# The opening of a two-block transformer kernel: pairs of feature blocks against one block at a time

## The reference, cut to what matters

```
mod = silu(c) @ w_mod + b_mod          # 6 x 1024: shift, scale, ... for x
mc  = silu(c_ctx) @ w_mod + b_mod      # the same for ctx
h   = rmsnorm(x, g_mix)   * (1 + mod[1]) + mod[0]
hc  = rmsnorm(ctx, g_mix) * (1 + mc[1])  + mc[0]
f   = h  @ w_in[:, 0:1024]             # forget gates of x, forward and backward
fc  = hc @ w_in[:, 0:1024]             # forget gates of ctx
```

## Time and profile before

| | |
|---|---|
| Time, median of 3 runs (lowest to highest) | 1463.91 us (1463.87 to 1466.01) |
| The profiled execution's own time | 1463.74 us |
| Its span (first to last instruction) | 1462.5 us |
| TensorE busy | 1433.3 us, 98% of the span |
| VectorE, ScalarE busy | 856.6 us (59%), 755.1 us (52%) |
| DMA | 267.34 MB, mean 183 GB/s |
| Mean granted clock of TensorE | 0.997 of full |

### The profile page before, as it was taken

The page is one execution under the profiler, slowest core; times in us unless marked ns, Lnnn a source line. Parts: engine busy times, 40 slices in busy tenths (PEclk is TensorE's granted clock), DMA queues, the critical chain, the costliest instruction groups (busy, mean ns, idle before and its releaser), DMA issues.

```text
span 1462.5 us, 19657 instructions
## 1 busy us (share of the span) xinstructions
PE 1433.3 (98%) x8098; PEld 1205.4 (82%) x8098; DVE 856.6 (59%) x1191; ACT 755.1 (52%) x1086; POOL 22.9 (2%) x72
## 2 busy tenths in 40 slices
PE   7999999999999999999999999999999999999998
PEld 5999889978888788888897888887888879888886
DVE  4628766875554755556355655557555475755553
ACT  4435355555453655445565655446455476755442
POOL 0000000000000000000121000000000000000000
PEclk9999999999999999999999999999999999999999
DMA  9437666555555555555433555565555552355552
GB/s 382 153 102 300 240 232 215 175 171 185 186 187 189 196 185 185 185 191 192 165 116 123 177 183 183 187 194 188 185 184 187 185 182 73 116 184 186 190 186 89
DMA packets 69930, 267.34 MB, mean 183 GB/s; under 512 B 7760, under 2 KB 8016, under 8 KB 66384
## 3 DMA queue, kind: packets, MB, share of 16 engines
q1 hardware_dynamic: 67680, 259.13, 52.7%
q10 hardware_dynamic: 2160, 6.95, 1.4%
HBM read 265.00 MB, written 1.05 MB: 182 GB/s over the span
## 4 chain that ended last, share of the span: by engine, by line
PE 91%; DVE 5%; ACT 2%; DMA 1%; issue 1%; SPq 0%; POOL 0%; DVEq 0%; ACTq 0%
PE PS L728 24%; PE PS L744 14%; PE PS L746 14%; PE PS L745 14%; PE PS L371 5%; PE PS L373 4%; PE PS L372 4%; PE PS L712 2%; PE PS L403 1%; PE PS L404 1%; PE PS L405 1%; DMA MC<-in_mod 1%; PE PS L472 1%; DVE WL L1652 1%; DVE TN L2099 1%
## 5 line engine op out<-in xcount | busy, mean ns | idle before, releaser
L1652 DVE TENSOR_TENSOR WL<-RAW,WH 128x1024 fp32r<-128x1024 f32 (+1 forms) x440 | 532.0, 1221 | 330.0 <-ACT WH L1093 329.5
L1093 ACT ACTIVATE WH<-RAW 128x1024 fp32r<-128x1024 f32 (+1 forms) x440 | 454.2, 1054 | 299.7 <-DMA RAW<-in_up 178.6
L744 PE MATMUL PS<-WH,XH 128*128 128x512 f32 (+1 forms) x928 | 380.9, 410 | 9.2 <-DVE XL L2107 9.0
L746 PE MATMUL PS<-WH,XL 128*128 128x512 f32 (+1 forms) x928 | 362.1, 390 | 0.0
L745 PE MATMUL PS<-WL,XH 128*128 128x512 f32 (+1 forms) x928 | 361.7, 390 | 0.0
L744 PEld LDWEIGHTS PS<-WH,XH 128*128 128x128 f32 x928 | 174.3, 188 | 59.5 <-DVE XL L2107 13.9
L746 PEld LDWEIGHTS PS<-WH,XL 128*128 128x128 f32 x928 | 174.2, 188 | 37.2
L745 PEld LDWEIGHTS PS<-WL,XH 128*128 128x128 f32 x928 | 175.0, 189 | 27.7
L728 PE MATMUL PS<-WH,GH 128*128 128x512 f32 x440 | 137.3, 393 | 0.0
L728 PE MATMUL PS<-WL,GH 128*128 128x512 f32 x440 | 135.8, 390 | 0.0
L728 PE MATMUL PS<-WH,GL 128*128 128x512 f32 x440 | 135.6, 389 | 0.0
(11 more groups left out here) (344 smaller groups left out, 1821.6 us busy)
## 6 DMA issues: line engine op xcount, KB each, us to landing
RAW<-in_up SPq DMA_DIRECT2D x220, 512.0 KB, 4.7
RAW<-in_down SPq DMA_DIRECT2D x110, 512.0 KB, 3.2
RAW<-in_win SPq DMA_DIRECT2D x44, 512.0 KB, 6.2
RAW<-in_mod SPq DMA_DIRECT2D x16, 1024.0 KB, 6.8
MC<-in_mod SPq DMA_DIRECT2D x8, 1024.0 KB, 13.6
RAW<-in_sbqk SPq DMA_DIRECT2D x16, 512.0 KB, 4.7
GROW<-in_grow ACTq DMA_DIRECT2D x9, 512.0 KB, 4.6
RAW<-in_wo SPq DMA_DIRECT2D x8, 512.0 KB, 4.1
```

Source lines behind the costliest of these rows:

```text
L744: e.matmul(o_[:, 0:n], l, w[:, s], start=(k == 0), stop=False, skip_group_check=True)
L746: m = e.matmul(o_[:, 0:n], ll, w[:, s], start=False, stop=(k == KD - 1), skip_group_check=True)
L1093: e.activation(WH[s][:, 0:c], RAW[s][:, 0:c], ACT.Copy).then_inc(*sig("hi", j))
L1652: e.tensor_tensor(WL[s][:, 0:c], RAW[s][:, 0:c], WH[s][:, 0:c].bitcast(F32), ALU.subtract).then_inc(*sig("lo", j))
```

## The change

The opening goes feature block by feature block. The columns of w_mod are reordered on the host so that modulation chunk k holds the shifts and the scales of feature block k: one chunk readies one block. The forget gates' weights become row chunks `("fg", k)`: all 1024 gate columns of feature block k. `gate_step(src, k, tiles)` multiplies block k into all four gate tiles, so x holds four PSUM banks through its eight steps; ctx follows, eight steps over four other banks. The weight chunk of step k is free after ctx's step k.

Squares are taken two blocks at a time, for x half by ACT and half by DVE. `sums` uses the squares as weights and two columns of ones as moving side, so a token's sum stands in its partition; `root` and `inverse_of` work on 4 columns; `spread` turns them to rows over all partitions with two matmuls, ACT copies those to `RB`. Normalising, gain and inverse root are one DVE operation (`scaled_x`), the shift is the bias of ACT's rounding (`halves`), and `low` recomputes it in one operation. TensorE takes modulation chunk k + 1 ahead of step k, and its turn between tiles 1 and 2 of step k; the sums of ctx stand in step 5, their spread in step 6. SP interleaves one modulation chunk and one weight chunk, the ctx read behind the fifth pair. Empty lines and most removed lines are left out here:

```diff
-    plan = [("win", i, 1024) for i in (0, 2, 1, *range(3, 20))]
+    plan = [("fg", k, 1024) for k in range(KD)] + [("win", i, 1024) for i in range(8, 20)]
...
-        FIRST = (4, 0, 5, 1, 6, 2, 7, 3)
+        FIRST = tuple(range(KD))
...
+        SQ = [ph("SQX", 32, [P, KD, T]), ph("SQC", 40, [P, KD, T])]
...
+            def gate_step(src, k, *tiles):
+                xh, xl, low = ((HH, HL, "hl"), (HCH, HCL, "hcl"))[src]
+                w, wl, split = weights("fg", k)
+                pe.wait_ge(*at(low, k))
+                pe.wait_ge(*split)
+                for i in tiles:
+                    name = ("fg", src, i)
                     if k == 0:
+                        b, empty = bank(name, ("fs", src, i))
                         pe.wait_ge(*empty)
                     b = BANK.of(name)
                     for t in range(2):
                         o_ = b[:, t * T:(t + 1) * T]
+                        c = slice(i * 256 + t * P, i * 256 + t * P + P)
                         e.matmul(o_, w[:, c], xh[:, k, :], start=(k == 0 and t == 0), stop=False, skip_group_check=True)
                         e.matmul(o_, w[:, c], xl[:, k, :], start=False, stop=False, skip_group_check=True)
                         m = e.matmul(o_, wl[:, c], xh[:, k, :], start=False, stop=(k == KD - 1), skip_group_check=True)
                     if k == KD - 1:
                         m.then_inc(*sig(*name))
+                    elif src and i == 3:
+                        m.then_inc(*sig("fgk", k))
+                if src:
+                    used[chunk["fg", k]] = ("fgk", k) if k < KD - 1 else ("fg", 1, 3)
...
+            def sums(nm, *parts):
+                b, empty = bank(("st", nm), ("act", "rs", nm))
+                pe.wait_ge(*empty)
+                for n, (engine, z) in enumerate(parts):
+                    pe.wait_ge(*at(engine, "sq", nm, z))
+                    for k in (2 * z, 2 * z + 1):
+                        for t in range(2):
+                            m = e.matmul(b[:, 2 * t:2 * t + 2], SQ[nm][:, k, t * P:(t + 1) * P], ONE[:, 0:2],
+                                         start=(n == 0 and k % 2 == 0 and t == 0), stop=(n == 3 and k % 2 == 1),
+                                         skip_group_check=True)
+                m.then_inc(*sig("st", nm))
+            def spread(nm):
+                b, empty = bank(("rx", nm), ("act", "rb", nm))
+                pe.wait_ge(*at("dve", "r", nm))
+                pe.wait_ge(*empty)
+                turned_rows(b, RS[nm][:, 0:4:2], 0, 2).then_inc(*sig("rx", nm))
...
+            sums(0, ("act", 0), ("dve", 2), ("act", 1), ("dve", 3))
             mod_first(0)
+            spread(0)
             mods_finish()
+            for k in range(KD):
+                if k < KD - 1:
+                    mod_first(k + 1)
+                if k == 5:
+                    sums(1, *(("act", z) for z in range(4)))
+                if k == 6:
+                    spread(1)
+                gate_step(0, k, 0, 1)
+                mods_finish()
+                gate_step(0, k, 2, 3)
+                if k == 0:
+                    for c in range(4):
+                        BANK.hold(("fg", 0, c))
+            for k in range(KD):
+                gate_step(1, k, *range(4))
+                if k == 0:
+                    for c in range(4):
+                        BANK.release(("fg", 0, c))
...
+            def squares(nm, src, ready, *parts):
+                ac.wait_ge(*ready)
+                for z in parts:
+                    e.activation(SQ[nm][:, 2 * z:2 * z + 2, :], src[:, 2 * z:2 * z + 2, :],
+                                 ACT.Square).then_inc(*sig("act", "sq", nm, z))
             def root(nm):
+                ac.wait_ge(*at("st", nm))
+                e.activation(RS[nm], BANK.of(("st", nm))[:, 0:4], ACT.Sqrt, bias=EPSV,
+                             scale=1.0 / D).then_inc(*sig("act", "rs", nm))
+            def rows_kept(nm):
+                ac.wait_ge(*at("rx", nm))
+                e.activation(RB[nm][:, :], BANK.of(("rx", nm))[:, 0:T], ACT.Copy).then_inc(*sig("act", "rb", nm))
+            def halves(k):
+                ac.wait_ge(*at("dve", "hn", k))
+                e.activation(HH[:, k, :], XF[:, k, :], ACT.Identity, bias=MOD[:, k, 0:1], scale=1.0).then_inc(*sig("hh", k))
+            def context_halves(k):
+                ac.wait_ge(*at("dve", "hcn", k))
+                e.activation(HCH[:, k, :], XC[:, k, :], ACT.Identity, bias=MOD[:, k, 1:2],
+                             scale=1.0).then_inc(*sig("hch", k))
...
+            squares(0, XF, (s_xf, 16), 0, 1)
             e.preload_act_table_set("sqrt_and_others")
+            root(0)
             mod_rows(0)
+            rows_kept(0)
+            for k in range(KD):
+                if k:
+                    mod_rows(k)
+                if k == 6:
+                    root(1)
+                if k == 7:
+                    rows_kept(1)
+                split(k)
+                halves(k)
+                if k == 4:
+                    squares(1, XC, (s_ctx, 16), 0, 1, 2, 3)
+            for k in range(KD):
+                context_halves(k)
             rows_in(0)
+            split(9)
+            for src, dst in enumerate((FX, FC)):
+                for c in range(4):
+                    ac.wait_ge(*at("fg", src, c))
+                    e.activation(dst[:, 2 * c:2 * c + 2, :], two(BANK.of(("fg", src, c))[:, :]),
+                                 ACT.Sigmoid).then_inc(*sig("fs", src, c))
+                split(14 + src)
...
+            def inverse_of(nm):
+                dv.wait_ge(*at("act", "rs", nm))
+                e.reciprocal(RS[nm], RS[nm]).then_inc(*sig("dve", "r", nm))
...
+            def scaled_x(k):
+                mod_added(k)
+                dv.wait_ge(*at("mod", k))
+                g = SM[:, S_GMIX + k:S_GMIX + k + 1].to_broadcast([P, 2])
+                e.scalar_tensor_tensor(VAC[:, k, :], MOD[:, KD + k, :], 1.0, g, ALU.add,
+                                       ALU.mult).then_inc(*sig("dve", "vac", k))
+                dv.wait_ge(*at("dve", "vac", k))
+                dv.wait_ge(*at("act", "rb", 0))
+                e.scalar_tensor_tensor(XF[:, k, :], XF[:, k, :], VAC[:, k, 0:1], RB[0][:, :], ALU.mult,
+                                       ALU.mult).then_inc(*sig("dve", "hn", k))
+            def scaled_context(k):
+                dv.wait_ge(*at("act", "rb", 1))
+                e.scalar_tensor_tensor(XC[:, k, :], XC[:, k, :], VAC[:, k, 1:2], RB[1][:, :], ALU.mult,
+                                       ALU.mult).then_inc(*sig("dve", "hcn", k))
+            def low(k):
+                dv.wait_ge(*at("hh", k))
+                e.scalar_tensor_tensor(HL[:, k, :], XF[:, k, :], MOD[:, k, 0:1], HH[:, k, :].bitcast(F32), ALU.add,
+                                       ALU.subtract).then_inc(*sig("hl", k))
+            def context_low(k):
+                dv.wait_ge(*at("hch", k))
+                e.scalar_tensor_tensor(HCL[:, k, :], XC[:, k, :], MOD[:, k, 1:2], HCH[:, k, :].bitcast(F32), ALU.add,
+                                       ALU.subtract).then_inc(*sig("hcl", k))
...
+            dv.wait_ge(s_xf, 16)
+            for z in (2, 3):
+                s = slice(2 * z, 2 * z + 2)
+                e.tensor_tensor(SQ[0][:, s, :], XF[:, s, :], XF[:, s, :], ALU.mult).then_inc(*sig("dve", "sq", 0, z))
+            inverse_of(0)
+            for k in range(KD):
+                if k:
+                    split(k)
+                if k == 6:
+                    inverse_of(1)
+                scaled_x(k)
+                if k == 0:
+                    split(0)
+                low(k)
+            for k in range(KD + 1):
+                if k < KD:
+                    scaled_context(k)
+                if k:
+                    context_low(k - 1)
...
+            split(9)
+            for src, dst in enumerate((FX, FC)):
+                for c in range(4):
+                    dv.wait_ge(*at("fs", src, c))
+                    for t in range(2):
+                        i = 2 * c + t
+                        e.tensor_scalar(dst[:, i, :], dst[:, i, :], OMLB(i), LB(i), ALU.mult,
+                                        ALU.add).then_inc(*sig("fm", src, i))
+                split(14 + src)
...
             e.dma_start(XF[:, :, :], a["xf"]).then_inc(s_xf, 16)
+            for k in range(KD):
+                modulation(k)
+                weights(k)
+                if k == 4:
+                    e.dma_start(XC[:, :, :], a["ctx"]).then_inc(s_ctx, 16)
+            for j in range(KD, len(plan)):
...
+    wmod = g["w_mod"][0]
+    wmod = np.concatenate([wmod[:, 0:2 * D].reshape(D, 2, KD, P).transpose(0, 2, 1, 3).reshape(D, 2 * D), wmod[:, 2 * D:]],
+                          axis=1)
...
-        "mod": cols(g["w_mod"][0], 256),
-        "win": cols(win, 256),
+        "mod": cols(wmod, 256),
+        "fg": rows(win[:, 0:1024]),
+        "win": cols(win[:, 1024:], 256),
```

(45 more changed lines are left out.)

137 lines of the change are left out of this document (13 added, 124 removed).

## The result

The changed kernel takes 1470.43 us (median of 4 runs, 1470.32 to 1472.58) against 1464.11 us for the kernel before in the same set of runs (1463.87 to 1466.01): 6.3 us more. The ratio is 1.0041, 95% interval 1.0029 to 1.0053. The forecast was 4.1 us more; its main case, "as summed, give or take 1.2 us", ended at 5.3. 1470.43 us is also just above the upper end of the stated range, 1470.2, which was worked out from 1463.91 us for the kernel before. The profiled execution took 1470.33 us, its span is 1469.1 us.

A forecast was written before the change was run, and what follows sets the result against it. TensorE, busy 98% of the span, bounds the kernel; the first token chunk's shift carries to the end. 20.9 + 61.2 + 1.3 + 1.4 = 84.8 us against 80.71: 4.1 us slower, 1468.0 us, range 1464.0 to 1470.2.

The forecast's parts named there:

- main case: Whole kernel: time as summed, 4.1 us slower at 1468.0 us, give or take 1.2 us; chance 0.52.
- the first gate matmul: End of the opening on TensorE: forget gates start at 20.9 us, 2.5 us earlier than in the kernel before.
- a return at 0.1 us: TensorE going from an fp32 group back to gate matmuls: 0.1 us extra each, 1.4 us in all.
- the wait of step 4: Step 4: ACT squares the context ahead of its copy of chunk 5, so TensorE's turn waits 0.55 us.
- the chain of a step: Readying step k+1 from its chunk on, through ACT and VectorE: 5.4 us, against 5.6 us of TensorE work.
- "clock": Rival, opening: two-column sums count as activity, full clock from 13 us, gates at 18.6, 1464.3 us; chance 0.14.
- "No extra for lone groups": Rival, x steps: chunks at 0.94 us and returns for nothing, 1.8 us less, 1466.2 us; chance 0.14.
- "chain too long": Rival, x steps: VectorE operations or hand-overs 0.1 us longer each, steps 4.8 us, 1469.5 us; chance 0.11.
- "supply": Rival, context steps: weight 14 lands late, ACT's sigmoid some 10 us late, time near 1477 us; chance 0.03.
- Half clock behind the first gate matmul: First gate matmuls run at half clock, as in the kernel before: 1.4 us.
- Context sums: Sums of the context, behind the first gate matmul: 3.7 us on TensorE, the full-clock length of 32 records.
- Wait of step 7: Ahead of step 7's gates, with no further chunk as cover: chain 5.95, work 5.15, TensorE waits 0.8 us.

The follow-up runs named there:

- run 4: Changed kernel with each x step's modulation chunk moved behind the turn (chunk k+2 in step k), one fp32 group per step: 1469.02 us, ratio 1.0034.
- run 1: Changed kernel with 128 instead of 2 moving columns of ones in both sums, x and ctx: 1465.11 us, ratio 0.9997 to the kernel before.
- run 3: Changed kernel with ACT and VectorE splitting the weights of step k+1 right behind step k: 1470.3 us, ratio 1.0038.
- Run 2: Changed kernel with 128 moving columns only in the sums of ctx, those of x keeping 2: 1468.36 us, ratio 1.0027.
- run 6: Changed kernel with 128 moving columns in the sums and seven constant-tile matmuls ahead of everything: 1462.97 us, ratio 0.9984.
- run 10: Kernel before, with seven constant-tile matmuls ahead and seven more in TensorE's wait for its third modulation chunk: 1464.08 us, ratio 0.9996.
- run 8: Kernel before, with seven constant-tile matmuls ahead of everything: 1465.66 us, ratio 1.0006.
- run 5: Changed kernel with seven unused constant-tile matmuls (256 moving columns) ahead of everything, two-column sums kept: 1468.05 us, ratio 1.0019.
- run 7: Run 6 with chunk 2 ahead of the first gate matmul, later chunks behind the turns, ctx spread in step 7, ctx squares in two parts: 1464.92 us.
- run 9: Run 6 with run 4's chunk order, the ctx spread in step 7 and ACT's copy behind step 7's rounding: 1462.40 us, ratio 0.9981.

## Why the prediction was right, and where it was short

The direction and the place came true; the main case, 4.1 us give or take 1.2, did not. Right by its steps: the place (everything ahead of the token chunks, carried unchanged to the end); the first gate matmul (20.9, 21.05 measured); half clock under the two-column sums, which decides that number; records of 0.216 and 0.115 us; the period of the x steps (4.6, measured 4.5 to 4.6); a return at 0.1 us (run 4); chunk and spread; the wait of step 4 (0.55, measured 5.04 minus 4.50). One sum is loose: the terms named for the chain of a step add up to 5.25 us, where 5.4 is stated; measured are 5.6, from the chunk at 26.84 to the gates that it serves, at 32.47. The rivals: "clock" did not come true in the kernel as it is, run 1 shows what it would have looked like: gates at 18.72 us against the 18.6 worked out for it, 1465.1 us against 1464.3. "No extra for lone groups" is refuted by run 4 and the lone chunks (1.00 us from start to gates, 26.84 to 27.84), "chain too long" by run 3, whose steps keep 4.50 us, and "supply" by the trace, in whose opening TensorE waits for no transfer. Chain's 1469.5 us is the forecast number nearest to the result, and by accident: its mechanism is not what made the time.

Short by 2.6 us at the token chunk (84.8 against 87.39), in three terms of the sum:

1. *Half clock behind the first gate matmul*, taken over as 1.4 us. The clock rose 5.1 us behind the first gate matmul, where in the kernel before it rose 3.3 us behind it: twenty of the 24 gates of step 0 and its turn ran at half clock. 21.05 to 26.84 is 5.8 us where 3.6 are due, 2.2 us. Off by 0.8.
2. *Context sums*, 3.7 us. Their own length was right. I had argued that two-column sums would not raise the clock and did not ask whether they would hold it; the term "3.7" should have been "3.7 and a half-clock spell behind it". Run 2 measures it as 1.5 us. This is the largest miss and one of thought, since its premise stands in the prediction.
3. *Wait of step 7*, 0.8 us. Measured 59.88 + 0.12 to 61.37, 1.4 us. The chain from chunk 7 to the gates took 6.24 us (55.13 to 61.37) instead of 5.95, mostly for the durations taken too short; TensorE's own work beside it took 4.87 us instead of 5.15. Each makes half of the miss.

These are 2.9 us; the remaining terms give 0.3 back.

The one sentence in which the prediction summed up its cause needs mending, though. It named the chunks, turns, returns and waits moved into the full stretch. Those are real by count, but they are not why the new order loses. With the clock kept full in both openings the new order reaches its token chunks at 78.66 us (run 6) and the old at 79.69 (run 10): what it moves behind the gates it gets back by starting them earlier. What makes the difference is the clock: full clock is worth 8.7 us to the new opening (87.39 to 78.66) and 1.0 us to the old (80.71 to 79.69). These are single executions, but the ratios agree: 1.0041 to 0.9984 is 8.3 us for the new kernel, and run 10's 0.9996 is 0.6 us for the old, not clear of zero. In the old one the half-clocked work lies beside waits for chunks (runs 8 and 10); in the new one it lies on the only path there is, sums, chunk, turn, gates.

How the 8.7 us divide depends on what is changed first. The columns alone bring 6.2 (run 1) and the seven matmuls ahead then 2.6. The seven matmuls alone bring 5.8 in the fastest execution of run 5 (81.59), and the columns then 2.9. So the half-clocked start and the two-column sums cost the same microseconds in part. And only the two changes together bring all of them in most executions: the median of run 5 is 5 us above that of run 6.

The Trainium skill (TensorE: Matmul & The Clock Gate, Part 4) says that transpose-mode matmuls do not count as busy time for the clock in the way others do. No run here tries that. What runs 1, 2 and 5 show is for fp32 matmuls with two moving columns, which are not in that mode: the clock did not rise during 6.9 us of them and fell behind 3.7 us of them, and with 128 columns in their place it rose and held. Part 1 of the same page of the Trainium skill, read as saying that an occupied engine is a fast engine, would have given 1464.3 us and was wrong here by 6 us.

## What to carry to other kernels

Before moving a reduction into a form with few moving columns because it costs the same time, ask what it does to TensorE's clock, both in its own place and for what follows: 128 columns took no longer at either clock and were worth some 6 us here. When something fills an engine's wait, look up when its input lands; three times here (runs 3, 7 and 9) a filled or removed wait came back, in part or whole, as another. And price half-clocked time only where it is on the path: the same half clock cost one opening 1 us and the other 8.7.

## What the runs showed of the hardware

- Records of fp32 matmuls with 128x128 weights start 0.11 us apart at full and 0.21 us apart at half clock, whether 2 or 128 columns move (full: 32 records in 3.71 us in run 5 and 3.81 us in run 6; half: the changed kernel with 2 columns, the first records of run 1 with 128).
- The clock shown in windows is 1.00 up to the first change that a trace records, also where it is half: in the changed kernel from 7.92 to 26.2 us, in the kernel before under the first sums (7.55 us on, twice as long a matmul as from 13.10 us on).
- ACT's rounding of 128x256 with a bias per partition takes 0.51 us; VectorE's operations with three operands 0.48 us for 256 columns.
- A half-clock spell can come late in the kernel, and does so in some executions only. From token chunk to end of span the traces have 1381.5 to 1381.8 us in eight kernels, 1382.8 in run 8 and 1383.0 to 1383.1 us in runs 1, 9 and 10. Apart from the openings and the last few us, exactly these four have a spell, all between 1184 and 1194 us, in or just behind a stretch in which TensorE waits; the other eight have that stretch too and no spell. Run 1's lies in this window, where the traces before and after show 1.00:

```profile
1190.00:1200.00 10.00, 9.94 (x56) 9.08 (x55) 6.57 (x19) 7.82 (x16) 0.00 (x0) 0.83 0.75 255
```

The Trainium skill (TensorE: Matmul & The Clock Gate, Part 1) says that the moment of such changes differs from run to run of the same kernel. One execution of each kernel was profiled, so no trace here shows it. The times of the kernel before lie in two groups, 1463.5 to 1464.9 and 1465.3 to 1466.8 us, and the mean granted clock is lower in the second (0.995 to 0.996 against 0.996 to 0.998). The groups lie about 2 us apart and the late spell costs 1.3, so it alone would not make them; what does was not tried.
